# A fifth unit of block 1 joins the dense product of a PEER layer

## The reference, cut to what matters

```python
cand = v1[..., :, None] + v2[..., None, :]            # 8 heads, 16 x 16 candidates
top_s, pos = lax.top_k(cand, PEER_TOPK)               # the best 16 of each head
idx = jnp.take_along_axis(cand_idx, pos, axis=-1)     # expert = i1 * 128 + i2
gate = jax.nn.softmax(top_s, axis=-1)
u, v = expert_u[idx], expert_v[idx]                   # rows of 2048
act = jax.nn.gelu(jnp.einsum('td,thkd->thk', tb, u), approximate=False)
return jnp.einsum('thk,thkd->td', gate * act, v)
```

## Time and profile before

| | |
|---|---|
| median of the timed runs | 1838.02 us |
| profiled execution | 1832.72 us |
| its span (first to last instruction) | 1830.9 us |
| PE, DVE, POOL, ACT busy | 80%, 72%, 49%, 24% of the span |
| DMA | 683.72 MB, mean 373 GB/s |
| gathers (queue q0) | 503.36 MB |
| plain transfers (queue q1) | 176.36 MB |
| dense product | 1283.7 to 1751 us |

### The profile page before, as it was taken

The page is one execution under the profiler, slowest core; times in us unless marked ns, Lnnn a source line. Parts: engine busy times, 40 slices in busy tenths (PEclk is TensorE's granted clock), DMA queues, the critical chain, the costliest instruction groups (busy, mean ns, idle before and its releaser), DMA issues.

```text
span 1830.9 us, 13641 instructions
## 1 busy us (share of the span) xinstructions
PE 1457.1 (80%) x4521; PEld 707.6 (39%) x4521; DVE 1311.3 (72%) x1684; ACT 435.1 (24%) x1160; POOL 891.4 (49%) x666
## 2 busy tenths in 40 slices
PE   5999999999999556655655666669999999989920
PEld 3434564575459312111111233345444444433300
DVE  3128877676138999999998787898556556556699
ACT  3012211120122222121223586687100000000000
POOL 0012233211006788888777787756455554322273
PEclk9999999999999766666667898979999999999965
DMA  9999989796658999999999999979999999999997
GB/s 364 378 361 342 352 334 326 300 348 244 221 186 345 380 418 420 418 418 420 419 419 417 405 406 391 381 291 386 414 413 412 413 413 413 381 418 417 417 422 312
DMA packets 164022, 683.72 MB, mean 373 GB/s; under 512 B 16433, under 2 KB 19057, under 8 KB 120689
## 3 DMA queue, kind: packets, MB, share of 16 engines
q0 software_dynamic: 92160, 503.36, 68.4%
q1 hardware_dynamic: 71360, 176.36, 25.5%
q10 hardware_dynamic: 432, 3.15, 0.4%
HBM read 678.51 MB, written 4.29 MB: 373 GB/s over the span
## 4 chain that ended last, share of the span: by engine, by line
DMA 35%; PE 28%; POOL 16%; DVE 14%; issue 5%; SPq 2%; ACT 0%; DVEq 0%; POOLq 0%; ACTq 0%
DMA arena<-in_expert_v,arena 27%; POOL arena L568 16%; DMA arena<-in_expert_u,arena 6%; PE PS L1807 6%; PE PS L1666 6%; PE PS L1567 5%; DVE arena L1382 5%; DVE arena L1425 3%; PE PS L1883 2%; DVE arena L1417 2%; PE PS L1548 2%; SPq L384 1%; PE PS L1523 1%; DMA arena<-in_w_mod 1%; DMA arena<-in_w_in 1%
## 5 line engine op out<-in xcount | busy, mean ns | idle before, releaser
L1382 DVE CUSTOM_DVE_ANT_0 arena<-arena 128x2048 f32<-128x2048 f32 x256 | 578.4, 2288 | 95.4 <-DMA arena<-in_expert_u,arena 94.4
L1883 PE MATMUL PS<-arena 128*128 128x512 f32 x512 | 364.1, 851 | 242.1 <-DMA arena<-in_expert_v,arena 242.0
L568 POOL DMA_INDIRECT arena<-in_expert_v,arena x256 | 401.9, 1570 | 285.8 <-DVE arena L1425 108.7
L568 POOL DMA_INDIRECT arena<-in_expert_u,arena x256 | 393.0, 1535 | 257.6 <-DVE arena L1357 89.5
L1935 PE MATMUL PS<-arena 128*128 128x512 f32 x1024 | 452.9, 600 | 16.3 <-DMA arena<-in_expert_v 14.2
L1935 PEld LDWEIGHTS PS<-arena 128*128 128x128 f32 x1024 | 192.7, 191 | 275.8 <-issue 227.4
L1883 PEld LDWEIGHTS PS<-arena 128*128 128x128 f32 x512 | 117.0, 253 | 456.4 <-DMA arena<-in_expert_v,arena 359.7
L1425 DVE SCALAR_TENSOR_TENSOR arena<-arena 128x2048 f32<-128x2048 f32 x62 | 145.8, 2351 | 56.9 <-DMA arena<-in_expert_v,arena 54.5
L1098 DVE SCALAR_TENSOR_TENSOR arena<-arena 128x1024 f32<-128x1024 f32 x120 | 160.9, 1341 | 25.7 <-DMA arena<-in_w_mod 22.9
L498 POOL DMA_DIRECT2D arena<-in_w_mod x128 | 68.8, 539 | 211.4 <-DVE arena L1098 180.7
L952 ACT ACTIVATE arena<-arena 128x4 f32<-128x4 f32 x64 | 13.0, 203 | 587.3 <-DVE arena L1382 516.2
(11 more groups left out here) (247 smaller groups left out, 1330.5 us busy)
## 6 DMA issues: line engine op xcount, KB each, us to landing
arena<-in_w_mod POOLq DMA_DIRECT2D x128, 512.0 KB, 7.3
arena<-in_expert_v SPq DMA_DIRECT2D x128, 512.0 KB, 8.0
arena<-in_w_mod SPq DMA_DIRECT2D x32, 1024.0 KB, 14.3
arena<-in_w_in SPq DMA_DIRECT2D x28, 1024.0 KB, 14.4
arena<-in_w_out SPq DMA_DIRECT2D x16, 1024.0 KB, 12.9
arena<-in_w_query SPq DMA_DIRECT2D x8, 1024.0 KB, 8.5
arena<-in_x SPq DMA_DIRECT2D x4, 1024.0 KB, 6.1
arena<-cum_rows SPq DMA_DIRECT2D x4, 1024.0 KB, 10.0
```

Of the source, the lines that this page charges most:

```text
L568: nc.gpsimd.indirect_dma_start(slot, None, table, bass.IndirectOffsetOnAxis(ap=rows[:, n:n + 1], axis=0),).then_inc(arrived, 16)
L1382: V.tensor_tensor_reduce(out=rows, in0=rows, in1=h2row[u // PH], scale=1.0, scalar=0.0, op0=ALU.mult, op1=ALU.add, accum_out=dots[:, u % B ...
L1883: ins = M(PS[:, b, :], diag_slot[m % DIAGS], slot[:, b * NQ:(b + 1) * NQ], start=(m == 0), stop=(m == BLK - 1))
```

## The change

One more unit, unit 12, enters the dense product: `DENSE` is 13 and `N_DENSE` 208. Its 16 slots need no right half of v any more, so they become 8 pairs of left halves instead of 16 full rows. There are 208 dots before the list of items, and the list has 136 items: 28 u, 40 that alternate between pair and u, 20 pairs and 48 full. Positions of the early v rows and of the batches of G are stretched or moved by 16.

Block 1 now has 80 slots in G. The first 64 stay stacked in halves. The slots of the fifth unit are copied four times, onto the quarters of the partitions (16 slots at partition 0, 32, 64 and 96). So eight groups of tokens (`QUARTERS`) take three batches of one-hots each: a batch for the quarters, that serves 16 tokens, and two for the halves of 8 tokens each, 24 batches in all. Each token takes two matmuls that accumulate in PSUM, one over 64 partitions and one over 16.

```diff
-DENSE = UNITS - 4
+DENSE = UNITS - 3
-LEFT = N_DENSE - BLK
+LEFT = BLK // 2
+MAIN = BLK + LEFT
-STACKED = BATCHES // 2
+QUARTERS = BATCHES // 4
+STACKED = 3 * QUARTERS
-ITEMS = [("u", N_DENSE + i) for i in range(20)]
+ITEMS = [("u", N_DENSE + i) for i in range(28)]
+ITEMS += [x for i in range(20) for x in (("pair", BLK + 2 * i), ("u", N_DENSE + 28 + i))]
+ITEMS += [("pair", BLK + 2 * i) for i in range(20, (N_DENSE - BLK) // 2)]
+ITEMS += [("full", N_DENSE + i) for i in range(3 * TOPK)]
-FEW, MANY = 15, 88
+FEW, MANY = 15, 84
-GAIN_AT, CLOSE_AT, RIGHT_AT = 124, len(ITEMS) - 16, len(ITEMS) - 8
+GAIN_AT, CLOSE_AT, RIGHT_AT = 112, len(ITEMS) - 6, len(ITEMS) - 3
+def first_token(q):
+    return (LEFT, 0, LEFT // 2)[q % 3] + BATCH * (q // 3)
+def banks_done(q):
+    return BATCHES + 4 * (q // 3) + (2 if q % 3 == 1 else 4)
...
                 elif i == 1:
-                    sp.wait_ge(g_ps, 2 * BATCHES - 4)
-                elif i == 2:
                     sp.wait_ge(g_ps, 2 * BATCHES)
...
-            for b in range(STACKED):
-                if b + 3 < STACKED:
-                    first_halves_stacked(b + 3)
-                if V_LATE + 2 + b < BLK:
-                    diagonal(V_LATE + 2 + b)
-                g_out(BATCHES + 2 * b)
-                g_out(BATCHES + 2 * b + 1)
+            for e in range(QUARTERS):
+                if e + 1 < QUARTERS:
+                    first_halves_stacked(3 * e + 3)
+                for b in (2 * e, 2 * e + 1):
+                    if V_LATE + 2 + b < BLK:
+                        diagonal(V_LATE + 2 + b)
+                    g_out(BATCHES + 2 * b)
+                    g_out(BATCHES + 2 * b + 1)
+                if e + 1 < QUARTERS:
+                    first_halves_stacked(3 * e + 4)
+                    first_halves_stacked(3 * e + 5)
...
+            def scatter_stacked(e, r):
+                last, q = 3 * e, 3 * e + 1 + r
+                pe.wait_ge(oh_dve, BATCHES + 2) if q == 1 else pe.wait_ge(oh_act, BATCHES + q - 1)
+                pe.wait_ge(oh2_dve, q + 1)
                 for h in range(2):
-                    bank_free(BATCHES + 2 * b + h)
-                    part = slice(h * LEFT, (h + 1) * LEFT)
+                    bank_free(BATCHES + 4 * e + 2 * r + h)
+                    part, rows = slice(h * LEFT, (h + 1) * LEFT), slice(32 * (2 * h + r), 32 * (2 * h + r) + TOPK)
                     for i in range(BATCH):
-                        ins = M(PS[:, 6 + h, i * P:(i + 1) * P], oh1[b % 4][part, i, :], oh2[b % 5][part, i, :], start=True, stop=True)
+                        to = PS[:, 6 + h, i * P:(i + 1) * P]
+                        M(to, oh1[q % 4][part, i, :], oh2[q % 5][part, i, :], start=True, stop=False)
+                        ins = M(to, oh1[last % 4][rows, i, :], oh2[last % 5][rows, i, :], start=False, stop=True)
...
+            for e in range(QUARTERS):
+                for r in range(2):
+                    scatter_stacked(e, r)
+                    if V_LATE + 2 * e + r < BLK:
+                        early_rows(V_LATE + 2 * e + r)
```

More of the change, by code:

```diff
@@ L61 @@
 V_LATE = 116
[L62 removed]
+V_POS = [20 + 110 * m // 62 if m < 62 else 130 + 73 * (m - 62) // 50 for m in range(V_EARLY)] + [203, 204, 206, 207]
 V_AT = {n: [m for m in range(V_LATE) if V_POS[m] == n] for n in range(N_DENSE + 16)}
 OH2_AT, OH1_AT, OUT_AT, G_AT = [{n + 7 * b // 4: b for b in range(BATCHES)} for n in (130, 133, 137, 143)]
[L65 to L71 removed]
+T_AT, T_ACT, DUP_AT, T_MORE, T_MORE_ACT = 134, 130, 194, 204, 203
+ROUTE_AT = {16 + 53 * (r - 2) // 4: r for r in range(2, UNITS)}
+ITEMS = [("u", N_DENSE + i) for i in range(28)]
[3 more added lines that the diff above has]
+FEW, MANY = 15, 84
 RING_OF = [k % 3 if k < FEW else (0, 1, 3, 4)[(k - FEW) % 4] if k < MANY else (0, 1, 3, 4, 5, 6, 7, 8)[(k - MANY) % 8] for k in range(len(ITEMS))]
@@ L197, in build @@
         e_twice = at(170, 4 * LEFT).rearrange("p (a s n) -> p a s n", a=2, s=2)
+        e_four = at(171, 2 * P).rearrange("p (a g n) -> p a g n", a=2, g=4)
+        coef_four = at(187.5, 896)[:, NCOL:NCOL + P].rearrange("p (g n) -> p g n", g=4)
         coef, idx = at(185, 2 * BLK), at(186, 2 * BLK).bitcast(U32)
@@ L888, in indices_twice @@
                 for a in range(2):
-                    ins = A(e_twice[:, a], e_all[:, a, BLK:N_DENSE].unsqueeze(1).to_broadcast([P, 2, LEFT]), ACT.Copy)
+                    A(e_twice[:, a], e_all[:, a, BLK:MAIN].unsqueeze(1).to_broadcast([P, 2, LEFT]), ACT.Copy)
+                    ins = A(e_four[:, a, :, 0:TOPK], e_all[:, a, MAIN:N_DENSE].unsqueeze(1).to_broadcast([P, 4, TOPK]), ACT.Copy)
                 ins.then_inc(slots_evac, 1)
             def stacked(dst, src):
-                A(dst[0:LEFT, 0:P // 2], src[0:LEFT, 0:P // 2], ACT.Copy)
-                return A(dst[LEFT:P, 0:P // 2], src[LEFT:P, P // 2:P], ACT.Copy)
+                A(dst[0:LEFT, 0:LEFT], src[0:LEFT, 0:LEFT], ACT.Copy)
+                ins = A(dst[LEFT:P, 0:LEFT], src[LEFT:P, LEFT:P], ACT.Copy)
+                for g in range(4):
+                    rows = slice(32 * g, 32 * g + 32)
+                    ins = A(dst[rows, LEFT:LEFT + 32], src[rows, P + 32 * g:P + 32 * g + 32], ACT.Copy)
+                return ins
             def slots_out_stacked():
@@ L1897, in coef_transpose, with twice_and_four @@
                 nc.tensor.transpose(PS[:, 3, 0:P], coef[:, 0:BLK], ident).then_inc(slots_ps, 1)
+            def twice_and_four(bank, first, twice, four):
+                nc.tensor.transpose(PS[:, bank, first:first + P], twice.rearrange("p s n -> p (s n)"), ident)
+                return nc.tensor.transpose(PS[:, bank, first + P:first + 2 * P], four.rearrange("p g n -> p (g n)"), ident)
             def slot_transposes_stacked():
@@ L1950, in _ @@
             coef_transpose_stacked()
-            for b in range(STACKED):
-                scatter_stacked(b)
-                if V_LATE + b < BLK:
-                    early_rows(V_LATE + b)
+            for e in range(QUARTERS):
[3 more added lines that the diff above has]
+                        early_rows(V_LATE + 2 * e + r)
             pe.wait_ge(g_evac, 2 * BATCHES)
```

28 lines of the change are left out of this document (13 added, 15 removed).

## The result

| | before | after |
|---|---|---|
| median of the timed runs | 1839.68 us (1836.51 to 1843.12, 4 runs) | 1980.01 us (1969.23 to 1983.51, 4 runs) |
| span of the profiled execution | 1830.9 us | 1979.2 us |
| DMA | 683.72 MB | 675.38 MB |

The account below looks back on a forecast made before the run. Bytes set the time while the DMA queues stay full. Dense product start 1372.6 + 467.2 - 6.8 gives 1833.0, plus 26.8 a span of 1859.8; with execution and median offsets, 1866 us, 28 slower, range 1834 to 1888.

Parts of the forecast that it names:

- The bytes and the 20 us they can win: Gathers and tiles fall from 480 to 472 MiB: 8.4 MB, at 418 GB/s 20 us, all the change can win.
- The order of the mechanisms: Longer building of G, then item 17's gather waiting for the last early row; dense product 112.4 us behind item 0.
- The failed step: Building of G for block 1: 15 shape changes within a step at 0.05 us each, 0.75 a step, 4.03 in all.
- The second failed step: Building of G: PE steps of 4.03 us, early rows of 1.92, groups of two steps 12.5.
- Rival C: Building of G: shape changes cost 0.1 to 0.2 us each, or PE's clock is lower; 1874 to 1891; chance 0.12.
- The stall at item 17: POOL issues item 17's gather only after the last early row; the gather takes 7.9 us to its dot, at 1347.3.
- The stretch behind the stall: Items 17 to 22 at 3.3 us each on DVE, 19.8 us; the dense product starts at 1372.6.
- The dense product and the end: Dense product 467.2 us, last 9 tiles at 3.42 us; then 26.8 us on DVE's path from block 0 complete.
- Item 0: Before the building of G: 16 more dots at 418 GB/s, 40.1 us, move item 0 from 1220.1 to 1260.2.
- Rival A: Building costs no more than its items, product starts at 1352, tiles keep PE's peak: 1811, median 1818; chance 0.11.

Follow-up runs that it names:

- the kernel without stacking: Against the changed kernel, block 1's 80 slots stand on 80 partitions, one product a token, 32 batches instead of 24: 1844.95 us, ratio 1.0027 to the kernel before.

## Why the prediction was wrong

**The bytes and the 20 us they can win: right.** 675.38 MB, and the gathers' queue has 8.4 MB less.

**The order of the mechanisms: right.** The building of G grows, the last early row comes later, item 17's gather waits for it and holds all of POOL, and the saved bytes don't pay for it. The dense product starts over 100 us behind item 0.

**The failed step: "between 64 and 16 partitions no row shows one; it lies between 0 and 0.1, I take 0.05".** Measured is 0.2 us at the full clock and 0.29 at the lower, so a step of 16 products takes 6.6 us at the full clock where I had 4.03. Two things went wrong. The row gave only half of the price, as the change into 64 partitions lengthens the interval on both sides of it. And from one small number I took a bound, where 240 changes hang on it: 0.05 gave 12 us a kernel, 0.2 gives 48. The Trainium skill (TensorEngine Tiling (Array Packing), Tiling Modes, Key Properties) says that a change of mode drains TensorE. The trace agrees in that a change has a price, 0.2 us; I had weighed the rule, and let the one row halve it.

**The second failed step: the forecast costed every step at the full clock.** It is the larger part. From the rows, as an estimate: 12 steps of 6.6 us with 12 early rows of 1.9 would have made about 102 us up to the last early row, 28 more than the 74.4 forecast; 165.2 were measured, and the other 63 are what the lower clock adds, with the dearer changes in it. Rival C had "0.1 to 0.2 us each time, or PE works at the lower granted clock", and ended at 1891. It is "and", not "or", and the clock lengthens all that PE does: 16 products at 0.22 are 3.5 us, with the changes 6.6 (0.415 each), and at the lower clock 11.5. The early rows doubled too, 1.92 to 3.7. I had taken them as given. Why the clock was low there stays open.

**The stall at item 17: right in kind, too small in size.** 8 to 16 us forecast, 33.8 measured: DVE had ended item 16 at 1410.3, and the last early row ended at 1438.3, two steps of 15 us with their early rows later. With three buffers for three more items the time behind item 0 fell by 13 only, as PE has to do the steps anyway.

**The stretch behind the stall: wrong bound.** I had DVE set it, at 3.3 us an item. PE did, with four steps of 11.5 us. By then DVE had done all 28 dots, where I had 23 items done at the start of the dense product.

**The dense product and the end: nearly right, for the reason given.** 458.1 against 467.2, just outside the 460 to 470 that I had named. The five more items that DVE had done ahead took 18 us off the way to item 130, and the tiles left over then ran at PE's peak, with DMA at 232 GB/s on average in 1920 to 1960 us, not under 200 (the last gathers still ran at its start). Full rows came every 3.76 us, close to the 3.79 of the earlier trace rows. DVE waited 35.3 us after item 130, forecast some 30. The turns of gathers and tiles, one gather for one tile, held here and in the kernels without stacking.

**Item 0: 8.4 us late.** About 3 us are the rate I took; the units' distance was tested and is not it, and the rest is open. A slip of 0.9 us in the forecast is small beside this: 1861.6 + 5.3 is 1866.9, not 1866.

**Rival A's picture**, that the building costs no more than its items, is nearly what the kernel without stacking shows (93.9 behind item 0 for A's 92). It still gains nothing, as the other half of A, tiles at PE's peak to the end, does not come.

## What to carry to other kernels

When a change puts two shapes of matmul in turn, count the changes and price each at 0.2 us or more until a row shows the interval before and behind one; not every change has a price (128 to 80 partitions had none). One matmul over more partitions can be cheaper than two accumulated ones that let more tokens share a batch: here 128 products over 80 partitions cost less than 256 over 64 and 16. Where PE is to become the bound of a stretch, work out its steps at both clocks, with the other costs as they are at each; a rival that has only one of them at a time is too narrow.

## What the runs showed of the hardware

- A change of a matmul's partitions between 64 and 16, or between 64 and 128, costs 0.20 us at the full clock (0.415 for 0.22 a product), and 0.29 at the lower one (0.72 for 0.43). From 128 to 80 it costs nothing that a row shows (1.82 us from early row to product, as with 128 throughout).
- With products over 16 partitions, in turn with 64 (231.9 us behind item 0) or alone (160.4), the granted clock was 0.50 to 0.67 in every window of 20 us of the building up to the stall, while PE was busy for 20.00 of 20 us. So idle time of PE isn't the reason in those windows. The same number of products over 64 partitions had 1.00 for 40 us, over 64 and 128 in turn 0.74 to 1.00, and both fell to 0.50 later. So small products go with the lower clock, but it comes without them too. It rests on one profile for each, and why it is so stays open.
- The share that gathers and tiles have of the queues did not depend on whether four or eight gathers were in flight (3.77 and 3.76 us for one of each).
